# A mixture-of-experts tail: order of the last two experts, sum of the last rows, and last norm

## The reference, cut to what matters

```python
g_w, g_idx = lax.top_k(softmax(xt @ w_rg + b_rg), 1)          # one of 4 groups
e_top, e_loc = lax.top_k(e_logits_of_that_group, 2)           # two of its 8 experts
y = (silu(x_e @ w_gate[e]) * (x_e @ w_up[e])) @ w_down[e]     # each expert, 1024 -> 512 -> 1024
ffn[token] += weight * y
x = x + gate2 * ffn
out = x * rsqrt(mean(x * x) + 1e-6) * g_final                 # the last norm, rows of 1024
```

## Time and profile before

| what | value |
|---|---|
| device time, median of 3 runs (lowest, highest) | 1056.23 us (1055.58, 1056.95) |
| profiled execution, its own time | 1057.68 us |
| its span | 1055.9 us |
| busy: TensorE, weight load, VectorE, ScalarE | 1029.4, 692.9, 505.6, 408.0 us |
| mean granted clock of TensorE over the span | 0.99 |
| DMA: bytes, mean rate | 327.89 MB, 311 GB/s |

### The profile page before, as it was taken

The page is one execution under the profiler, slowest core; times in us unless marked ns, Lnnn a source line. Parts: engine busy times, 40 slices in busy tenths (PEclk is TensorE's granted clock), DMA queues, the critical chain, the costliest instruction groups (busy, mean ns, idle before and its releaser), DMA issues.

```text
span 1055.9 us, 13811 instructions
## 1 busy us (share of the span) xinstructions
PE 1029.4 (97%) x5646; PEld 692.9 (66%) x5646; DVE 505.6 (48%) x713; ACT 408.0 (39%) x644; POOL 22.2 (2%) x42
## 2 busy tenths in 40 slices
PE   9999999999999999999999999999999999999985
PEld 6888878888999999898897544444444444434332
DVE  5676677987977755766665412121112121111112
ACT  6734634446444434664844222222222222212112
POOL 1000000010000000100000000000000000000000
PEclk9999999999999999899999999999999999999988
DMA  9977548976888653474255999999999999999992
GB/s 331 391 266 242 195 156 289 320 256 230 293 312 296 240 198 122 142 261 156 96 200 230 367 423 421 421 421 420 420 421 421 421 422 421 421 421 421 421 419 93
DMA packets 86467, 327.89 MB, mean 311 GB/s; under 512 B 5776, under 2 KB 5936, under 8 KB 61696
## 3 DMA queue, kind: packets, MB, share of 16 engines
q1 hardware_dynamic: 85056, 323.45, 79.3%
q0 software_dynamic: 1344, 3.50, 1.0%
HBM read 325.88 MB, written 1.05 MB: 310 GB/s over the span
## 4 chain that ended last, share of the span: by engine, by line
PE 48%; DMA 8%; DVE 1%; issue 1%; ACT 1%; DVEq 0%; ACTq 0%
PE bank L1025 18%; PE bank L1048 9%; PE bank L1061 3%; DMA raw<-in_w_expert_up 3%; DMA es<-in_w_expert_up 3%; PE bank L993 3%; DMA e_wlo<-in_w_expert_up 2%; PE bank L580 2%; PE bank L583 2%; PE bank L586 2%; PE bank L1034 1%; PE bank L550 1%; PE bank L556 1%; PE bank L553 1%; PE bank L1007 1%; PE bank L1009 1%
## 5 line engine op out<-in xcount | busy, mean ns | idle before, releaser
L1600 DVE TENSOR_TENSOR wlo<-raw,whi 128x2048 fp32r<-128x2048 f32 x87 | 199.0, 2290 | 95.9 <-ACT whi L1114 95.5
L1114 ACT ACTIVATE whi<-raw 128x2048 fp32r<-128x2048 f32 x87 | 165.9, 1912 | 95.9 <-PE bank L556 38.6
L2221 DVE SCALAR_TENSOR_TENSOR YS<-bank,wsl,gate2q 128x512 f32<-128x512 f32 x32 | 24.0, 751 | 217.6 <-PE bank L1048 217.6
L1025 PE MATMUL bank<-raw,XT 128*64 128x512 f32 x360 | 119.8, 597 | 0.0
L1025 PE MATMUL bank<-es,XT 128*64 128x512 f32 x328 | 113.9, 606 | 4.4 <-DMA es<-in_w_expert_up 3.4
L553 PE MATMUL bank<-wlo,hh 128*128 128x512 f32 x224 | 87.5, 391 | 1.6 <-DVE wlo L1600 1.4
L550 PE MATMUL bank<-whi,hh 128*128 128x512 f32 x224 | 88.1, 393 | 0.4 <-ACT whi L1121 0.4
L556 PE MATMUL bank<-whi,hl 128*128 128x512 f32 x224 | 87.3, 390 | 0.0
L1025 PEld LDWEIGHTS bank<-es,XT 128*64 128x64 f32 x328 | 34.2, 139 | 74.2 <-issue 73.2
L1025 PE MATMUL bank<-e_whi,XT 128*64 128x512 f32 x168 | 76.1, 596 | 2.7 <-DMA e_wlo<-in_w_expert_up 2.7
L1025 PE MATMUL bank<-e_wlo,XT 128*64 128x512 f32 x168 | 76.2, 596 | 0.0
(11 more groups left out here) (382 smaller groups left out, 1955.1 us busy)
## 6 DMA issues: line engine op xcount, KB each, us to landing
raw<-in_w_in SPq DMA_DIRECT2D x41, 1024.0 KB, 6.2
raw<-in_w_expert_up SPq DMA_DIRECT2D x33, 1024.0 KB, 22.5
raw<-in_w_ff SPq DMA_DIRECT2D x32, 1024.0 KB, 5.3
es<-in_w_expert_gate SPq DMA_DIRECT2D x31, 1024.0 KB, 22.4
raw<-in_w_ada SPq DMA_DIRECT2D x24, 1024.0 KB, 6.0
e_whi<-in_w_expert_gate SPq DMA_DIRECT2D x21, 1024.0 KB, 23.2
e_wlo<-in_w_expert_up SPq DMA_DIRECT2D x21, 1024.0 KB, 25.3
es<-in_w_expert_down SPq DMA_DIRECT2D x21, 1024.0 KB, 26.0
```

What stands on the lines that cost most here:

```text
L1025: m = e.matmul(b[64 * w:64 * w + 64, :], K.XT[j // 4 % 2][:, k, j % 4, :], K.weights(halves[w])[:, 512 * c:512 * c + 512], start=k == 0, s ...
L1114: e.activation(whi[n % RING][:, :], raw[h.raw][:, :], ACT.Copy).then_inc(S["hi"], 1)
L1600: e.tensor_tensor(wlo[n % RING][:, :], raw[h.raw][:, :], whi[n % RING][:, :].bitcast(F32), ALU.subtract).then_inc(S["lo"], 1)
```

## The change

1. In `order_weights`, TensorE's, ScalarE's programs and the bank plan, the first half of expert 31's gate and up stands ahead of the down projection of expert 30, so that TensorE's steady order holds up to there; then come `gate_up(31,1)`, `combine(30)`, `middle(31)`, two filler matmuls into a free bank, `down(31)` and `combine(31)`.
2. The last expert's rows are not split: no `YH` and `YL`, and `combine(31)` multiplies the fp32 `YS` by the fp32 view of `PT`, four matmuls instead of eight. The waits that counted `yl` are adapted (`parted`).
3. The last norm: VectorE multiplies each bank by the norm's factors into `fin` while ScalarE squares the other bank of the same rows; then, for both t, reciprocal, and half of each row scaled by VectorE and half by ScalarE. The output is stored in two DMAs of 512 KB instead of four of 256 KB.
4. The loads of `bgb` and `nfb` increment the semaphore `l_ws` of three earlier loads, and every wait on it, or on the two removed semaphores, is for all five.
5. ScalarE and VectorE read the count of overflow blocks at expert 28 instead of after expert 31.

```diff
--- before.py
+++ after.py
@@ -291,10 +291,10 @@
 
         for base, n, one in ((0, NE, fixed), (NE, NOV, moving)):
             for j in range(n + 1):
-                if j == n - 1:
-                    one(j - 1, 2, 0)
-                    one(j - 1, 2, 1)
                 for hf in range(2 if j < n else 0):
+                    if j == n - 1 and hf:
+                        one(j - 1, 2, 0)
+                        one(j - 1, 2, 1)
                     one(j, 0, hf)
                     one(j, 1, hf)
                 if j > 0 and j != n - 1:
@@ -336,6 +336,10 @@
     def landed(self, h, c):
 
         return (self.S[f"first{c // 2}"], 16) if h.i == 0 else (self.S[f"raw{h.raw}"], h.loaded)
+
+    def parted(self, j):
+
+        return j if j < NE else j - 1
 
     def weights(self, i):
 
@@ -475,12 +479,6 @@
                 use(f"gat{p0}_{q}", ((1, 2, 3, 1)[q], f"xt{q % 2}", 4 * p0 + q // 2 * 2 + 2))
             for j in range(base, base + n + 1):
                 p, q = j // 4 + 1, j % 4
-                if j == base + n - 1:
-                    use(f"hid{j - 1}", (2, "hf", j))
-                    use(f"down{j - 1}", (3, "ys", j))
-                    use(f"gu{j}", (j % 2, "GU", j + 1))
-                    use(f"turn{j}", (3, "pt", 4 * j + 4))
-                    continue
                 if j < base + n:
                     use(f"gu{j}", (j % 2, "GU", j + 1))
                 if j == 2:
@@ -495,6 +493,7 @@
                     use(f"down{j - 1}", (3, "ys", j))
 
         block_uses(0, NE)
+        use("busy", (0, "GU", NE - 1))
         block_uses(NE, NOV)
 
 
@@ -611,7 +610,7 @@
     def mix_a(t):
         e.wait_ge(S["vn"], 2)
         e.wait_ge(S["ws_z"], 1)
-        e.wait_ge(S["l_ws"], 48)
+        e.wait_ge(S["l_ws"], 80)
         for q in range(2):
             free(f"mixa{t}{q}")
             b = K.at[f"mixa{t}{q}"][0]
@@ -1052,14 +1051,20 @@
 
         def combine(j):
 
+
             e.wait_ge(S["pt"], 4 * j + 2)
-            e.wait_ge(S["yl"], j + 1)
+            whole = j == base + n - 1
+            if whole:
+                e.wait_ge(S["ys"], j + 1)
+            else:
+                e.wait_ge(S["yl"], K.parted(j) + 1)
             for t in range(2):
-                for y in (K.YH, K.YL):
+                for y in (K.YS,) if whole else (K.YH, K.YL):
                     for q in range(2):
                         r = slice(64 * q, 64 * q + 64)
-                        m = e.matmul(K.at[f"moe{2 * t + q}"][0][:, :], K.PT[j % 4][r, 128 * t:128 * t + 128], y[r, :],
-                                     start=False, stop=j == base + n - 1 and y is K.YL, skip_group_check=True)
+                        pt = K.PT[j % 4][r, 128 * t:128 * t + 128]
+                        m = e.matmul(K.at[f"moe{2 * t + q}"][0][:, :], pt.bitcast(F32) if whole else pt, y[r, :],
+                                     start=False, stop=whole, skip_group_check=True)
                 m.then_inc(S["comb" if t else "comb_t0"], 1)
 
         for q in range(4):
@@ -1083,14 +1088,16 @@
             if j > base:
                 down(j - 1)
         j = base + n - 1
-        middle(j - 1)
-        down(j - 1)
         gate_up(j, 0)
         turn_p(j)
+        middle(j - 1)
         combine(j - 2)
+        down(j - 1)
         gate_up(j, 1)
         combine(j - 1)
         middle(j)
+        if base == 0:
+            stay_busy(2, "busy")
         down(j)
         combine(j)
 
@@ -1495,7 +1502,7 @@
             e.wait_ge(S["turnP"], j + 1)
             if j > 3:
                 e.wait_ge(S["comb"], j - 3)
-                e.wait_ge(S["yl"], j - 3)
+                e.wait_ge(S["ys"], j - 3)
             for r in (slice(0, 64), slice(64, 128)):
                 e.activation(K.PT[q][r, :], b[0:64, 0:256], ACT.Copy).then_inc(S["pt"], 1)
             for r in (slice(0, 64), slice(64, 128)):
@@ -1535,18 +1542,17 @@
         gathered(base // 4, 1)
         gathered(base // 4, 3)
         count = None
-        for j in range(base, base + n + 2):
-            if j == NE:
+        for j in range(base, base + n + 1):
+            if j == NE - 4:
                 e.wait_ge(S["ovf"], 1)
                 count = e.value_load(K.ovf[0:1, 0:1], min_val=0, max_val=NOV - 1)
-            if base + 1 < j != base + n:
+            if base + 1 < j < base + n:
                 down(j - 2)
-            if j < base + n - 1:
+            if j < base + n:
                 turned_p(j)
-            if base < j <= base + n:
+            if base < j:
                 middle(j - 1)
             if j == base + n - 1:
-                turned_p(j)
                 down(j - 1)
             if j < base + n:
                 if j % 2 and 4 * (j // 4 + 1) < base + n:
@@ -1565,9 +1571,16 @@
     for t in range(2):
         e.wait_ge(S["comb" if t else "comb_t0"], NE)
         for n in range(2):
+            if n:
+                e.wait_ge(S["fin"], 2 * t + 1)
             e.activation(K.sqx[:, t, 512 * n:512 * n + 512], K.at[f"moe{2 * t + n}"][0][:, :], ACT.Square,
                          scale=1.0 / 32, accum_out=stat(8 * t + n)).then_inc(S["sq"], 1)
-        root(10 + t, 8 * t, 1)
+        if t:
+            root(10, 0, 1)
+    root(11, 8, 1)
+    for t in range(2):
+        e.wait_ge(S["rs"], 10 + t)
+        e.activation(K.fin[:, t, 512:1024], K.fin[:, t, 512:1024], ACT.Copy, scale=stat(8 * t)).then_inc(S[f"out{t}"], 1)
 
 
 def dve_program(e, K):
@@ -1721,7 +1734,7 @@
             e.scalar_tensor_tensor(out=dst[:, t, o], in0=K.at[use][t][:, :], scalar=stat(t), in1=K.bgb[:, q],
                                    op0=ALU.mult, op1=ALU.add).then_inc(S["gr"], 1)
 
-    e.wait_ge(S["l_bgb"], 16)
+    e.wait_ge(S["l_ws"], 80)
     gate_out("ga0", 10, K.ga, 0, 0)
     lo(24)
     lo(25)
@@ -1832,7 +1845,7 @@
     e.wait_ge(S["a1"], 1)
     e.tensor_tensor(K.a1[:, :], K.a1[:, :], K.vec[:, VEC["g_nf"]:VEC["g_nf"] + 8], ALU.mult).then_inc(S["a1"], 1)
     e.wait_ge(S["st"], ST_AT["1"] + 2)
-    e.wait_ge(S["l_nfb"], 16)
+    e.wait_ge(S["l_ws"], 80)
     e.wait_ge(S["zl"], 16)
     for t in range(2):
         for n in range(2):
@@ -2218,9 +2231,13 @@
         def down(j):
             e.wait_ge(S["eused"], K.half_of[j, 2, 1] + 1)
             e.wait_ge(S["pt"], 4 * j + 4)
+            if j > base:
+                e.wait_ge(S["yl"], K.parted(j))
             e.scalar_tensor_tensor(out=K.YS[:, :], in0=K.at[f"down{j}"][0][:, :], scalar=K.wsl[:, j % 4:j % 4 + 1],
                                    in1=K.gate2q[:, :], op0=ALU.mult, op1=ALU.mult).then_inc(S["ys"], 1)
-            e.wait_ge(S["yh"], j + 1)
+            if j == base + n - 1:
+                return
+            e.wait_ge(S["yh"], K.parted(j) + 1)
             e.tensor_tensor(K.YL[:, :], K.YS[:, :], K.YH[:, :].bitcast(F32), ALU.subtract).then_inc(S["yl"], 1)
 
         one_hots(base // 4)
@@ -2271,20 +2288,36 @@
 
     e.wait_ge(S["comb_t0"], NE)
     e.wait_ge(S["l_gfb"], 16)
-    for t in range(2):
+
+    def gained(t, n):
+        if n == 0:
+            e.wait_ge(S["sq"], 29 + 2 * t)
+        e.tensor_tensor(K.fin[:, t, 512 * n:512 * n + 512], K.at[f"moe{2 * t + n}"][0][:, :],
+                        K.gfb[:, 512 * n:512 * n + 512], ALU.mult).then_inc(S["fin"], 1)
+
+    def mean(t):
         k = 8 * t
-        if t:
-            e.wait_ge(S["comb"], NE)
         e.wait_ge(S["sq"], 30 + 2 * t)
         e.scalar_tensor_tensor(out=stat(k), in0=stat(k), scalar=EPS, in1=stat(k + 1), op0=ALU.add,
                                op1=ALU.add).then_inc(S["ms"], 1)
+
+    def scaled(t):
+        k = 8 * t
         e.wait_ge(S["sd"], 10 + t)
         e.reciprocal(stat(k), stat(k)).then_inc(S["rs"], 1)
         e.wait_ge(S["rs"], 10 + t)
-        for n in range(2):
-            o = slice(512 * n, 512 * n + 512)
-            e.scalar_tensor_tensor(out=K.fin[:, t, o], in0=K.at[f"moe{2 * t + n}"][0][:, :], scalar=stat(k),
-                                   in1=K.gfb[:, o], op0=ALU.mult, op1=ALU.mult).then_inc(S["fin"], 1)
+        e.wait_ge(S["fin"], 2 * t + 2)
+        e.tensor_scalar(K.fin[:, t, 0:512], K.fin[:, t, 0:512], stat(k), None, ALU.mult).then_inc(S[f"out{t}"], 1)
+
+    gained(0, 1)
+    gained(0, 0)
+    mean(0)
+    e.wait_ge(S["comb"], NE)
+    gained(1, 1)
+    gained(1, 0)
+    mean(1)
+    scaled(0)
+    scaled(1)
 
 
 def pool_program(e, K):
@@ -2313,9 +2346,9 @@
     e.wait_ge(S["raw2"], 16)
     e.dma_start(K.gvb[:, :], A["norm_v_g"].broadcast_to([128, 1024])).then_inc(S["l_ws"], 16)
     e.wait_ge(S["raw4"], 16)
-    e.dma_start(K.bgb[:, :], A["b_gate"].broadcast_to([128, 2048])).then_inc(S["l_bgb"], 16)
+    e.dma_start(K.bgb[:, :], A["b_gate"].broadcast_to([128, 2048])).then_inc(S["l_ws"], 16)
     e.wait_ge(S["raw5"], 16)
-    e.dma_start(K.nfb[:, :], A["norm_final_g"].broadcast_to([128, 1024])).then_inc(S["l_nfb"], 16)
+    e.dma_start(K.nfb[:, :], A["norm_final_g"].broadcast_to([128, 1024])).then_inc(S["l_ws"], 16)
     for g in range(7):
         ada_start(g)
     e.wait_ge(S["m"], 4)
```

(8 more changed lines are left out.)

## The result

| kernel | median us (lowest, highest; runs) | profiled execution, its span |
|---|---|---|
| before | 1055.32 (1054.30, 1057.89; 13) | 1057.68, 1055.9 |
| after | 1053.55 (1052.83, 1055.36; 13) | 1053.28, 1051.5 |

The ratio is 0.9982 [0.9975, 0.9990]: 1.9 us faster, with an interval of 1.1 to 2.6. 1053.4 was predicted. The two profiled executions lie 4.4 apart, which is far more: before's is one of its slowest executions, after's an ordinary one.

A forecast was written before the change was run, and what follows sets the result against it. Expert-weight DMA bounds until about 1030 us, then TensorE, then the last norm. Order -2.2, combine -1.5, norm +0.8 give -2.9 against the profiled 1057.68; from the median 1056.23 the forecast is 1053.4, range 1051.3 to 1055.6.

The forecast's parts named there:

- order, to `gate_up(31,1)`: TensorE at experts 30 and 31: second-half gate and up of 31 start at 1031.95 instead of 1034.16, 2.2 us earlier.
- fillers: Gap before down(31): two filler matmuls take 0.86 to 0.92, fit the 0.98 gap, cost nothing; uncovered, up to 0.9.
- last combine: Combine of expert 31: dropping YH and YL saves 1.39, fp32 halves at once 0.1 more; 1.5 gained (1.05 to 1.5).
- norm and stores: Last norm to final landing: 0.8 us longer (0.3 to 1.3), 9.0 from the first square instead of 8.2.
- The wait of 0.8 for slot 189: Before `gate_up(31,1)`: 31's second-half up load lands at 1031.8, so TensorE, free at 1031.2, gives back 0.8 of 3.0.
- 1.9 of fall: down(30) after the 2.03 stop: slower clock makes 16 matmuls take 5.35 instead of 3.46; this 1.9 counted as gone.
- the first pair 0.64: Last combine: two fp32 halves of 64 rows run at once, first pair out after 0.64, 0.1 less than before.
- less than 8.5 a failure: Last norm: stores land 9.0 after the first square; landing within 8.5 would show the forecast wrong.
- B: Rival: last loads later for TensorE or fp32 halves not at once; 1054.8, or -0.6 with fillers on the path; chance 0.25.
- C: Rival: stores overlap, scalings fast, norm costs 0.1 or less, slot 189 in time; -3.7 to -4.4, 1052.2; chance 0.16.
- D: Rival: new stops bring TensorE to 1.2 GHz for the rest, 1.9 more per 16 matmuls; +2.8, 1059.0; chance 0.04.
- E: Rival: slot 185 stays the latest landing and every stop only moves; within 0.5 of before, 1056.0; chance 0.05.

The follow-up runs named there:

- a1: The changed kernel run again, unaltered: 1053.55 us against 1055.41 for before, ratio 0.9983.
- a4: Kernel before with two filler matmuls in its 2.03 us stop before down(30), nothing else: 1055.65 us against 1055.41, ratio 1.0001.
- b2: Kernel before with only the last expert's rows summed unsplit in fp32: 1053.84 us against 1055.20, ratio 0.9985.
- b3: Kernel before with only the new last norm and its two 512 KB stores: 1056.72 us against 1055.20, ratio 1.0009.
- c1: Kernel before with two fillers in each of two stops, the load wait near 1005 and before down(30): 1054.46 us against 1055.30, ratio 0.9992.
- b1: Kernel before with only the new order of loads and last two experts; split combine, old norm, no fillers: 1054.61 us against 1055.20, ratio 0.9993.
- a2: The changed kernel without its two filler matmuls: 1052.70 us against 1055.41 for before, ratio 0.9977.
- c2: a2 with two fillers in the wait for expert 30's loads near 1005: 1052.99 us against 1055.30 for before, ratio 0.9979.
- a3: The changed kernel with the old last norm and four 256 KB stores: 1053.72 us against 1055.41 for before, ratio 0.9983.
- d1: a2 with the steady order to the end, both halves of 31's gate and up before down(30): 1051.90 us against 1055.30 for before, ratio 0.9970.
- d2: d1 with 31's transposes between the halves of down(30) and down(31) in another bank: 1051.07 us against 1055.48 for before, ratio 0.9957.
- b4: a2 with the combine of expert 30 split around the transposes of 31: 1053.01 us against 1055.20 for before, ratio 0.9977.

## Why the prediction came out

**The time was right, partly by luck: every term of the sum was off, by 0.5 to 0.7 us, and the errors cancel.** The forecast said -2.2 for the order, -1.5 for the combine, +0.8 for the norm and nothing for the fillers. In after's trace they are, in the same units:

| step | predicted | measured |
|---|---|---|
| order, to `gate_up(31,1)` | -2.2 | -2.9 (27.9 to 25.0) |
| fillers | 0 | +0.7 |
| last combine | -1.5 | -1.0 |
| norm and stores | +0.8 | +0.1 |
| sum | -2.9 | -3.1 |

The traces' own sum can be made from one common point: 1006.28 to the end of the span is 49.6 in before, 1004.97 to the end is 46.5 in after, so -3.1. The other 1.3 of the 4.4 between the two executions lies ahead of these points, where the change has only parts 4 and 5. Much of it begins at the very start, shown by the first eight matmuls of before and then of after:

```profile
1.60 6.19 PE L596 MATMUL bank<-gate1b 128*128 128x512 f32 x8 [1.60 <-DVE gate1b L1622]
```

```profile
1.60 5.18 PE L595 MATMUL bank<-gate1b 128*128 128x512 f32 x8 [1.60 <-DVE gate1b L1635]
```

6.19 and 5.18 for the same work. In before they start 0.85 apart up to the sixth and 0.43 apart from the seventh on, in after the distance changes behind the fourth: a factor of two, like the two levels of the clock, though the row of the granted clock reads 1.00 here in both. Of this 1.0, 0.75 is left when ScalarE rounds weights at 48.93 and 48.18, and by 451.83 and 450.50 it has grown to 1.33: near 440 the granted clock is 0.50 for a stretch in both. a1 began as slowly as before did (6.32 for the first eight) and was level with after by then. Part 4 costs nothing in it: in after the first use behind the joined semaphore starts 0.20 behind VectorE's reciprocal, as in before. So this 1.3 is put down to chance between executions, which is argued and not shown.

**The order.** The stop before `gate_up(31,0)` was 0.3 as predicted, down(30)'s 0.43 where 0.5 stood, and no fall followed either. The wait of 0.8 for slot 189 was wrong. After issued it at 1002.73, it took 27.1, so it landed at 1029.8, 10.1 behind slot 185, where I had 10.7 from before's two rows. TensorE came at 1030.00, 0.2 behind it. Working from the landing times was right, but the 10.7 was an exception: outside before's trace and a4's the two slots land 9.9 to 10.3 apart, and with that no wait is left. What sets the 25.0 in all the kernels with after's order is slot 185: it lands 14.9 behind the loads of expert 30's first half, and from `gate_up(31,0)` to `gate_up(31,1)` TensorE needs 10.1.

**What the order is worth depends on the execution, and that the prediction missed.** The stretch to `gate_up(31,1)` is 27.9 with the old order in the three traces with both falls (before, b2, b3: 5.35 for each group of 16), 25.3 where none comes (c1), and 25.0 with the new order, whether the clock fell at 1005 (after, b1, a2) or not (a1, c2). a4's 26.0, also without a fall, holds 0.66 of waiting for its late slot 189; without it, it would be 25.3 too, and if the landing does not depend on the order, the new order would have waited for it as well. So by the traces the new order is worth 2.9 in an execution with both falls and 0.3 in one without; an execution of the old order with one fall is not among the traces. I took before's profiled execution for a typical one, and counted 1.9 of fall as always there. Its mean granted clock was 0.990; of 102 runs of before, the 20 at 0.990 or less have a median of 1057.3 and the other 82 of 1055.05. The mean clock also counts stretches at 0.50 that cost little or nothing here (near 440, and behind TensorE's last matmul), so it is a rough sign of the falls near 1006 and 1023: of the traces with both, b2's has 0.992 and b3's 0.989. b1's 0.6 is what remains on average; 0.5 that its last combine lost in the trace may be in it. That the forecast of the median nevertheless came true is luck, a second pair of errors that cancel: it took 2.9 from 1056.23, the median of three runs of before. Over the 13 runs beside after that median is 1055.32, 0.9 lower, and the gain is 1.8, 1.1 smaller. The same sum from 1055.32 would have given 1052.4.

**The fillers.** "Two take 0.86 to 0.92" was the wrong step. The row of six matmuls in 2.74 is of three calls, for one fp32 call is recorded as two matmuls. Two calls are the chain's x4, 1.72. So they did not fit into the gap of 0.98, and 0.7 went on the path, close to the "up to 0.9" without cover. a2 shows it and shows that nothing is lost without them. The calls in the code (`stay_busy(3, ...)`) have to be counted against the count in the row.

**The combine.** The same error made the first pair 0.64: an fp32 call of 64 rows is recorded twice as well, and the first four recorded matmuls take 1.14, for both banks of t=0. It is in the reading of the earlier trace rows too. The experts' matmuls are fp32; a `gate_up` half or a `down` is 8 calls in the code, not 16, recorded as 16, so the 3.58 are four pairs of calls and not eight, and 0.64 is the length of one record, half a call. That the halves run at once was right: four one behind the other would take 1.7. The gain is 1.0, not 1.5, in after; b2 measured 1.0 in its trace, and 1.4 by its medians or 1.6 by its ratio. The Trainium skill's page "FP8 and Floating Point Precision" (TensorE Precision Notes) says that true fp32 makes four passes through the array. The trace agrees: an fp32 call of 512 columns takes 0.86, where fp32r ones of 512 columns, recorded once each, start 0.23 apart, as in before's first block:

```profile
100.14 0.40 PE L550 MATMUL bank<-whi,hh 128*128 128x512 f32 x1
100.37 0.39 PE L553 MATMUL bank<-wlo,hh 128*128 128x512 f32 x1
```

**The norm.** The scalings took 0.48 instead of 0.75, so the last store was issued 4.6 after the first square and not 5.4. The Trainium skill's page "VectorE: DVE Perf Modes" (Mode 2x_2P), which I had weighed and set aside for a 128x128 row, was right in its direction: by it I had estimated 0.55. The last landing came 4.3 behind the first issue (1046.76 to 1051.08), where I took 4.5 (4.2 to 5.0). The estimate of 4.4 from "DMA: Bandwidth & Descriptors" is as near, but that section of the Trainium skill is written of DMAs that GpSimd issues, and these stores are SyncE's. The last landing came 8.3 behind the first square, and my own text had called less than 8.5 a failure of this step: it is one. Before's last store took 2.8, as I took it, and landed 8.2 behind the first square: so the mis-sized part is the new norm's, 8.3 and not 9.0. From the first square to the end of the span it is 8.64 before and 8.73 after. The scatter of the stores is larger than that difference (9.1 in b3, 9.0 with the old norm in a3), and a3's median says zero.

**The rivals.** B asked for a later slot 189 and fp32 halves one behind the other, and neither was so, though its side remark of fillers on the path was. C named the right size of the norm (0.1) and a slot 189 in time, which are both what happened; it missed because of the fillers and of the combine's doubled records. D did not happen: no clock fell after the stops of 0.30 and 0.43. E is half right: the landing of slot 185 does set the new stretch, but at 25.0 and not at before's 27.9, and the medians moved by 1.9.

**What stays open.** The single effects (order 0.7, sum 1.0 to 1.5, norm 0, fillers -0.7) add up to 1.0 to 1.5, against 1.9 [1.1, 2.6] of the whole; within their intervals that is no contradiction. Parts 4 and 5 of the change were never run alone, and part 5 has no reading of its own. Whether a split combine behind its 2.3 us stop runs at half clock more often than not, which the unsplit one with its short stop avoids, rests on b1's one trace. b3's 0.9 has no cause that the runs show.

## What to carry to other kernels

Before a gain is read from one profiled execution, its own time is to be placed among the runs: if it is at their upper end, what it shows of falls of the clock may be worth its full price only in the executions that have them. Where a wait for a load stands behind a slow stretch, the wait absorbs it; look for the last stretch that no load ends, and shorten that, as the version with the transposes inside the down projection did. Count the calls in the code against the count in a row before dividing its time.

## What the runs showed of the hardware

- The granted clock after an idle piece of TensorE is not given by its length alone. Near 1005 the matmuls ran at 1.2 GHz for a part behind eight stops of 2.50 to 3.12 (before, after, a2, b1, b2, b3, d1, d2) and at 2.4 GHz throughout behind four of 2.16 to 2.71 (a1, a3, a4, b4); 2.71 stands on both sides (b2; a1 and a3). Behind the stop of 2.03 near 1022 they were slow in all three traces that have it (before, b2, b3). With two fillers in the stop they stayed at 2.4 GHz each time (a4 near 1020, c1 at both places, c2 near 1005).
- One fp32 call of 512 columns took 0.86 on 128 rows (1.72 for the two fillers, recorded as four matmuls), an fp32r one 0.23 (recorded once). Two fp32 calls on halves of 64 rows run at once: four recorded matmuls in 1.14 up to the end of the last, where one behind the other they would need 1.7.
- VectorE's fp32 scaling by a column of 128x512 from SBUF to SBUF took 0.48, that of 128x128 0.339: the larger tile costs 0.14 more for four times the elements. A scaling from the accumulator bank with a second input (YS) took 0.75 to 0.76 for 512 elements.
